# First pair's attention: the high parts of the queries of heads 2 to 7 made by VectorE in place of ScalarE

## The chip, the cores and the metric

One core of a Trainium2 chip runs the whole program. The engines are TensorE (PE in the profile, its weight loads PEld), VectorE (DVE), ScalarE (ACT), GpSimd (POOL) and SyncE (SP), which issues most transfers. The metric is the device time of one execution in microseconds (us), as the median of several.

## The reference

Two blocks follow each other. The first has two layers ("the first pair"), the second two others. Only the attention of the first block is touched. It is a window attention over 512 tokens, in row blocks of 128, with 8 query heads of 64 channels and 2 key heads; each row block sees itself, its neighbours and 256 context rows. In layer 0 the 256 context rows are updated too, so they are two more row blocks of queries.

```python
def window_attention(q, k, v, kc, vc, sink_b):
    ...
        s_loc = jnp.einsum('bqkgd,bnkd->bkgqn', qi, ks).astype(jnp.float32)
        s_loc = jnp.where(valid, s_loc, -jnp.inf)
        s_ctx = jnp.einsum('bqkgd,bnkd->bkgqn', qi, kc).astype(jnp.float32)
        p = sink_softmax(jnp.concatenate([s_ctx, s_loc], axis=-1), sink_b).astype(v.dtype)
        return (jnp.einsum('bkgqn,bnkd->bqkgd', p[..., :nc], vc)
                + jnp.einsum('bkgqn,bnkd->bqkgd', p[..., nc:], vs))
```

Beside the attention each layer has a Fourier mix and a short convolution ("the sides"), which are gated and merged with the attention's output by `w_out`.

## The kernel before

The program is written by hand, one instruction stream for each engine, with semaphores between them. The order of the streams is the order of the code; nothing is scheduled. Matrix products keep nearly fp32 precision: each operand is split into a high part (rounded to the type fp32r) and a low part (the rest), and three products are added. For weights ScalarE makes the high part (`w_hi`, line 874) and GpSimd the low part (`w_lo`, line 800).

In the attention the queries of a head lie on 64 partitions of `q1` (a part of `qk`). For the scores both parts of a head's queries are put in one buffer of 128 partitions, `q_parts[h % 2]`: the high part on its own 64 partitions, the low part on the other 64. There are two such buffers, so head h is written when the scores of head h - 2 are done. A head's queries are 64 x 768 in layer 0 (six row blocks) and 64 x 512 in layer 1 (four).

The attention is a pipeline over steps, one row block of one head (a unit) a step: `n_q` is 6 in layer 0 and 4 in layer 1, so there are 48 and 32 units. At step s TensorE makes the scores of unit s (line 1504), transposes the probabilities of unit s - 3 (line 1523) and multiplies unit s - 4 with the values (line 1539). VectorE at its step st adds mask and takes the minimum for unit st (`scored`, lines 2203 and 2205; TensorE makes the scores of unit s + 2 in the same PSUM region only after it), scales the output of unit st - 5 (line 2224), takes a reciprocal (line 2214), and then does what `side_lo` lists for the step. ScalarE at each step copies the transposed probabilities to `pt` (line 935; TensorE's next transposes use the same PSUM region and wait for it), takes the exponential of a unit (`exp1`, line 922), and then does what `between` lists.

Those two lists are what the change touches. In `between` ScalarE made the high part of head h = step // n_q + 2 at the last step of a head (`q_hi`, line 916), behind a wait for the scores of that step. In `side_lo` VectorE makes the low part of head st // n_q + 1 at the first step of a head (`q_lo`, line 2473), from head 2 on: steps 6, 12, 18, 24, 30, 36 in layer 0, and 4, 8, 12, 16, 20, 24 in layer 1. `SIDE_STEPS` is (10, 14, 18, 22): at these steps ScalarE makes the high part of one side (`h_hi`, line 1163), and two steps later, at 12, 16, 20 and 24, VectorE makes its low part (`h_lo`, line 2191), behind `q_lo` where both fall on a step. At steps 24, 26, 28 and 30 ScalarE also splits weights (`w_hi`), and GpSimd follows with `w_lo`. GpSimd's other work in the attention is the Fourier gate (lines 815 to 822, `fpair` and `gf`), at its start.

Heads 0 and 1 get their parts before the loop, from ScalarE (`q_hi`) and VectorE (`q_lo`), in both kernels.

Of the kernel before, what the change touches and what calls it, by code (L numbers as in the profile page):

```python
# [14 lines left out]
F32 = mybir.dt.float32  # L15
F32R = mybir.dt.float32r
ALU = mybir.AluOpType
# [10 lines left out]
HD = 64  # L28
EPS = 1e-6
HEADS, KVH = 8, 2  # L30
# [104 lines left out]
def _program(nc, I, out, seen):  # L135
    ctx = ExitStack()
    with ctx:
# [216 lines left out]
        s_q0_landed = Signal(nc, ctx, seen, "q0_landed")  # L354
        s_q_hi = Signal(nc, ctx, seen, "q_hi")
        s_q_lo = Signal(nc, ctx, seen, "q_lo")
        s_q_rot = Signal(nc, ctx, seen, "q_rot")
        s_recip = Signal(nc, ctx, seen, "recip")
        s_resid = Signal(nc, ctx, seen, "resid")
# [498 lines left out]
        def _(act):  # L858
# [53 lines left out]
            def q_hi(l, h):  # L912

                b = HD * (h % 2)
                n = TOK if l < DEPTH - 1 else SEQ
                act.activation(q_parts[h % 2][b:b + HD, 0:n], q1[b:b + HD, h // 2, 0:n], ACT.Copy).then_inc(s_q_hi.sem, s_q_hi.nth((l, h)))
# [104 lines left out]
            for l in range(DEPTH):  # L1021
# [125 lines left out]
                exp1(l, units, 3)  # L1147

                def between(step):
                    h = step // n_q + 2  # L1150
                    if step % n_q == n_q - 1 and h < HEADS:
                        act.wait_ge(s_scores.sem, s_scores.at((l, step)))
                        q_hi(l, h)
                    if step == SIDE_STEPS[0]:
                        act.wait_ge(s_fmix.sem, s_fmix.at((l, "ctx") if both else (l, 1)))
                    if step in SIDE_STEPS:
                        c = SIDES[SIDE_STEPS.index(step)]
                        if c < 2:
                            act.wait_ge(s_fgate.sem, s_fgate.at((l, c)))
                        else:  # L1160
                            act.wait_ge(s_side.sem, s_side.at((l, c)))
                        src = gf[:, c, 0:nc_] if c < 2 else cb[:, c - 2, 0:nc_]
                        act.activation(h_hi[:, 4 + c, 0:nc_], src, ACT.Copy).then_inc(s_hi.sem, s_hi.nth((l, "s", c)))
                    if step in (24, 28):
                        split_next((0,))
                    if step in (26, 30):
                        split_next((1,))
# [1008 lines left out]
        def _(dve):  # L2176
            V = nc.vector
# [210 lines left out]
            for l in range(DEPTH):  # L2388
# [80 lines left out]
                def q_lo(h):  # L2469
# [3 lines left out]
                    V.tensor_tensor(q_parts[h % 2][HD - b:2 * HD - b, 0:nc_], q1[b:b + HD, h // 2, 0:nc_],  # L2473
                                    q_parts[h % 2][b:b + HD, 0:nc_].bitcast(F32), ALU.subtract).then_inc(s_q_lo.sem, s_q_lo.nth((l, h)))

                cw, bias = VB[l]["conv_w"], VB[l]["conv_b"]
                for c in range(2):
                    tap = [vec_t[:, cw + 2 * j + c:cw + 2 * j + c + 1] for j in range(3)]
# [42 lines left out]
                def side_lo(st):  # L2521

                    if st == 8:
                        summed_in((5, 7)[l])
                        if l == 1:
                            gate_vector(1)

                    if st > 0 and st % n_q == 0 and st // n_q + 1 < HEADS:
                        q_lo(st // n_q + 1)
                    if st in (2, 3):  # L2530
                        mixed_out(st - 2)
                    if st == 3 and both:
                        dve.wait_ge(s_fmix.sem, s_fmix.at((l, "ctx")))
                        V.tensor_copy(fmix[:, :, SEQ:], ps[:, 2, :].rearrange("p (c n) -> p c n", c=2)).then_inc(s_fm_out.sem, s_fm_out.nth((l, "ctx")))
                    if st - 2 in SIDE_STEPS:
                        c = SIDES[SIDE_STEPS.index(st - 2)]
                        src = gf[:, c, 0:nc_] if c < 2 else cb[:, c - 2, 0:nc_]
                        lo_part(h_lo[:, 4 + c, 0:nc_], src, h_hi[:, 4 + c, 0:nc_], (l, "s", c), (l, "s", c))
# [304 lines left out]
```

## Time and profile before

| | us |
|---|---|
| runs | 1903.93, 1906.1, 1907.13 |
| median | 1906.1 |
| the profiled execution's own time | 1902.68 |
| its span | 1900.4 |
| TensorE busy | 1866.1 |
| ScalarE busy | 820.9 |
| VectorE busy | 794.0 |
| GpSimd busy | 714.5 |

The span goes from the first to the last instruction of the profiled execution; its own time is 2.3 us longer. TensorE's granted clock is 0.998 of full speed over the span. The attention of layer 0 lies between about 242 and 322 us of the span, that of layer 1 between about 540 and 603.

### The profile page before, as it was taken

The page shows a single profiled execution, that of the slowest core. Times are in us where ns is not written, and L with a number is a line of the kernel's source. Part 1 is how long each engine was busy: PE and PEld are TensorE (multiplying, and loading weights), DVE is VectorE, ACT ScalarE, POOL GpSimd, SP SyncE. Part 2 cuts the span into 40 slices and gives each one's busy share as a digit, 9 for nine tenths or more (in the row PEclk, how much of TensorE's full clock was granted, in tenths as well). Part 3 has the DMA queues.
Part 4 walks back from the last instruction along what each step waited for, and adds up shares of the span by engine and source line. Part 5 has one row for each costly group of instructions (what it writes and reads, how often), then busy time and mean ns, then how long its engine had stood idle before and what let it go on. Part 6 is the DMA issues. An engine that isn't in the chain of part 4 may idle for free.

```text
span 1900.4 us, 28008 instructions
## 1 busy us (share of the span) xinstructions
PE 1866.1 (98%) x10996; PEld 1576.8 (83%) x10996; DVE 794.0 (42%) x1801; ACT 820.9 (43%) x1577; POOL 714.5 (38%) x567
## 2 busy tenths in 40 slices
PE   8999999999999999999999999999999999999997
PEld 6888878878878888888988888888888898888886
DVE  4585585276465363775311110056277541111003
ACT  5222386472276474873323222127487342232212
POOL 2433221255512453204544445444420355444452
PEclk9999999999999999999999999999999999999999
DMA  9554412125311233102333333223320232332321
GB/s 328 199 143 147 142 24 68 56 74 175 111 24 54 85 102 119 63 1 90 89 105 95 89 111 111 101 88 97 107 84 1 89 89 89 110 91 90 132 89 44
DMA packets 198321, 185.70 MB, mean 98 GB/s; under 512 B 27246, under 2 KB 165636, under 8 KB 198192
## 3 DMA queue, kind: packets, MB, share of 16 engines
q1 hardware_dynamic: 183640, 172.52, 28.8%
q10 hardware_dynamic: 14552, 11.40, 2.1%
q8 instruction: 89, 1.46, 0.3%
q14 instruction: 40, 0.33, 0.1%
HBM read 179.11 MB, written 5.44 MB: 97 GB/s over the span
## 4 chain that ended last, share of the span: by engine, by line
PE 90%; ACT 3%; DVE 2%; POOL 2%; issue 1%; SPq 1%; DMA 1%; DVEq 0%; ACTq 0%
PE ps L1444 25%; PE ps L1446 24%; PE ps L1445 24%; PE ps L2053 3%; PE ps L1969 3%; PE ps L1504 2%; PE ps L1539 2%; PE ps L1523 2%; PE ps L2071 2%; POOL w_lo L800 2%; PE ps L1465 1%; ACT w_hi L874 1%; DMA raw<-in_w_mod 1%; SPq L768 0%; ACT pt L935 0%
## 5 line engine op out<-in xcount | busy, mean ns | idle before, releaser
L800 POOL TENSOR_TENSOR w_lo<-raw,w_hi 128x512 fp32r<-128x512 f32 (+1 forms) x505 | 667.6, 1353 | 1072.0 <-ACT w_hi L874 1071.9
L874 ACT ACTIVATE w_hi<-raw 128x1024 fp32r<-128x1024 f32 (+3 forms) x255 | 252.1, 1034 | 250.4 <-PE ps L1446 191.0
L1444 PE MATMUL ps<-g_hi,w_lo 128*128 128x512 f32 (+1 forms) x928 | 348.4, 375 | 1.4 <-POOL w_lo L800 1.4
L1445 PE MATMUL ps<-g_lo,w_hi 128*128 128x512 f32 (+1 forms) x928 | 347.5, 374 | 0.0
L1446 PE MATMUL ps<-g_hi,w_hi 128*128 128x512 f32 (+1 forms) x928 | 347.4, 374 | 0.0
L1444 PEld LDWEIGHTS ps<-g_hi,w_lo 128*128 128x128 f32 x928 | 174.7, 188 | 33.7 <-issue 1.7
L1445 PEld LDWEIGHTS ps<-g_lo,w_hi 128*128 128x128 f32 x928 | 174.7, 188 | 31.2
L1446 PEld LDWEIGHTS ps<-g_hi,w_hi 128*128 128x128 f32 x928 | 174.7, 188 | 31.2
L2798 DVE TENSOR_TENSOR tmp_f<-ps,tmp_f 128x512 f32<-128x512 f32 x44 | 30.4, 692 | 370.3 <-PE ps L1446 370.3
L1444 PE MATMUL ps<-h_hi,w_lo 128*128 128x512 f32 (+1 forms) x496 | 177.1, 357 | 2.3 <-DVE h_lo L2191 2.3
L1445 PE MATMUL ps<-h_lo,w_hi 128*128 128x512 f32 (+1 forms) x496 | 174.6, 352 | 0.0
L1446 PE MATMUL ps<-h_hi,w_hi 128*128 128x512 f32 (+1 forms) x496 | 174.5, 352 | 0.0
L1444 PE MATMUL ps<-w_hi,hid_lo 128*128 128x512 f32 x352 | 137.1, 390 | 0.0
L1446 PE MATMUL ps<-w_hi,hid_hi 128*128 128x512 f32 x352 | 136.9, 389 | 0.0
L1445 PE MATMUL ps<-w_lo,hid_hi 128*128 128x512 f32 x352 | 136.9, 389 | 0.0
L1399 ACT ACTIVATE hid_hi<-tmp_f 128x512 fp32r<-128x512 f32 x44 | 27.8, 632 | 237.2 <-DVE tmp_f L2798 237.2
L2756 DVE SCALAR_TENSOR_TENSOR res<-res,ps 128x512 f32<-128x512 f32 x32 | 21.8, 685 | 231.6 <-PE ps L1446 231.4
L1444 PE MATMUL ps<-w_hi,g_lo 128*128 128x512 f32 (+3 forms) x320 | 114.2, 357 | 1.5 <-POOL w_lo L800 1.5
L1446 PE MATMUL ps<-w_hi,g_hi 128*128 128x512 f32 (+3 forms) x320 | 112.0, 350 | 0.0
L1445 PE MATMUL ps<-w_lo,g_hi 128*128 128x512 f32 (+3 forms) x320 | 111.7, 349 | 0.0
L1444 PEld LDWEIGHTS ps<-h_hi,w_lo 128*128 128x128 f32 x496 | 93.8, 189 | 21.0 <-issue 8.8
L1446 PEld LDWEIGHTS ps<-h_hi,w_hi 128*128 128x128 f32 x496 | 93.8, 189 | 12.8
(294 smaller groups left out, 3328.3 us busy)
## 6 DMA issues: line engine op xcount, KB each, us to landing
raw<-in_w_in SPq DMA_DIRECT2D x33, 1024.0 KB, 5.0
raw<-in_w_mod SPq DMA_DIRECT2D x24, 1024.0 KB, 6.5
raw<-in_w_gate SPq DMA_DIRECT2D x44, 512.0 KB, 3.6
raw<-in_w_up SPq DMA_DIRECT2D x44, 512.0 KB, 4.7
raw<-in_w_down SPq DMA_DIRECT2D x22, 1024.0 KB, 4.7
raw<-in_w_out SPq DMA_DIRECT2D x8, 1024.0 KB, 5.3
strips<-bias_rows ACTq DMA_DIRECT2D x18, 256.0 KB, 3.2
raw<-in_w_o SPq DMA_DIRECT2D x4, 1024.0 KB, 4.8
```

Source lines behind the costliest of these rows:

```text
L800: pool.tensor_tensor(w_lo[:, i % SPLIT, a:e], raw_of(what)[:, a:e], w_hi[:, i % SPLIT, a:e].bitcast(F32), ALU.subtract).then_inc(s_tile_lo ...
L874: act.activation(w_hi[:, i % SPLIT, a:b], raw_of(what)[:, a:b], ACT.Copy).then_inc(s_tile_hi.sem, s_tile_hi.nth((what, n)))
L1444: pe.matmul(o, lhs[1], rhs[0], start=first, stop=False)
L1445: pe.matmul(o, lhs[0], rhs[1], start=False, stop=False)
L1446: return pe.matmul(o, lhs[0], rhs[0], start=False, stop=last)
L1504: m = pe.matmul(ps_flat[:, o0 + CTX + col:o0 + CTX + col + k.shape[1]], q, k, start=j == 0, stop=j == len(products) - 1)
L1523: m = pe.transpose(ps_flat[:, o0 + P * j:o0 + P * j + P], s_[:, i % n_b, P * j:P * j + P], ident[:])
L1539: m = pe.matmul(ps_flat[q_, o0:o0 + HD], turned, v, start=j == 0, stop=j == n - 1)
L1969: pe.matmul(ps[:, b, 0:u["n"]], u["q"], u["k"], start=True, stop=True).then_inc(s_scores.sem, s_scores.nth((y, i)))
L2053: m = pe.matmul(ps[:, b, 0:HD], pt2[r % N_P][:, P * j:P * j + P], v, start=j == 0, stop=j == len(u["vs"]) - 1)
L2071: m = pe.transpose(ps[:, b, P * j:P * j + P], probs_of(i)[:, P * j:P * j + P], ident[:])
L2798: V.tensor_tensor(tmp_f[:, 2 + j % 2, :], ps[:, 2 * ((j + 2) % 4) + 1, :], tmp_f[:, j % 2, :], ALU.mult).then_inc(s_glu.sem, s_glu.nth((y, ...
```

## The change

ScalarE no longer makes the high parts of heads 2 to 7, in both layers. VectorE makes them, right ahead of the low part: it waits for the scores of the head before (`s_scores` of unit n_q x (h - 1) - 1), copies the queries to fp32r, waits for its own copy (a new semaphore, `later_q_hi`), and subtracts. The low part was released by ScalarE's semaphore before. The low part's instruction is the same.

```diff
@@ -1147,10 +1148,6 @@
                 def between(step):
-                    h = step // n_q + 2
-                    if step % n_q == n_q - 1 and h < HEADS:
-                        act.wait_ge(s_scores.sem, s_scores.at((l, step)))
-                        q_hi(l, h)
                     if step == SIDE_STEPS[0]:
@@ -2473,6 +2470,16 @@
+                def later_q(h):
+
+                    b = HD * (h % 2)
+                    own, other = slice(b, b + HD), slice(HD - b, 2 * HD - b)
+                    dve.wait_ge(s_scores.sem, s_scores.at((l, n_q * (h - 1) - 1)))
+                    V.tensor_copy(q_parts[h % 2][own, 0:nc_], q1[own, h // 2, 0:nc_]).then_inc(s_later_q_hi.sem, s_later_q_hi.nth((l, h)))
+                    dve.wait_ge(s_later_q_hi.sem, s_later_q_hi.at((l, h)))
+                    V.tensor_tensor(q_parts[h % 2][other, 0:nc_], q1[own, h // 2, 0:nc_],
+                                    q_parts[h % 2][own, 0:nc_].bitcast(F32), ALU.subtract).then_inc(s_q_lo.sem, s_q_lo.nth((l, h)))
@@ -2526,7 +2533,7 @@
                     if st > 0 and st % n_q == 0 and st // n_q + 1 < HEADS:
-                        q_lo(st // n_q + 1)
+                        later_q(st // n_q + 1)
```

VectorE's queue at step 12 of layer 0, where head 3 is prepared; before (`ISA` is the reduction with the mask or the reading of its accumulator; `L2191` is the low part of a side):

```order
L2205 ISA sc,small<-ps,band_first,sinks 128x512
L2205 ISA small 128x1
L2224 TENSOR_SCALAR ao_113<-ps,small 128x64
L2214 RECIPROCAL small<-small 128x1
L2473 TENSOR_TENSOR q_parts_112<-qk,q_parts_112 64x768
L2191 TENSOR_TENSOR h_lo<-cb,h_hi 128x768
L2203 COPY sc<-sinks 128x1
L2205 ISA sc,small<-ps,band_mid,sinks 128x640
```

and of the change (the same lines of code stand 3 lines further up or 7 further down in it):

```order
L2202 ISA sc,small<-ps,band_first,sinks 128x512
L2202 ISA small 128x1
L2221 TENSOR_SCALAR ao_113<-ps,small 128x64
L2211 RECIPROCAL small<-small 128x1
L2478 CAST q_parts_112<-qk 64x768
L2480 TENSOR_TENSOR q_parts_112<-qk,q_parts_112 64x768
L2188 TENSOR_TENSOR h_lo<-cb,h_hi 128x768
L2200 COPY sc<-sinks 128x1
L2202 ISA sc,small<-ps,band_mid,sinks 128x640
```

A CAST of 64x768 stands ahead of the low part; everything behind it, `h_lo` and the reduction of unit 13 first, is one instruction further back.

ScalarE's queue over the steps 10 to 12 of layer 0, before:

```order
L1163 ACTIVATE h_hi<-cb 128x768
L935 ACTIVATE pt<-ps 128x640
L922 ACTIVATE sc,small<-sc,small 128x257
L916 ACTIVATE q_parts_112<-qk 64x768
L935 ACTIVATE pt<-ps 128x512
L922 ACTIVATE sc,small<-sc,small 128x513
```

and of the change:

```order
L1160 ACTIVATE h_hi<-cb 128x768
L936 ACTIVATE pt<-ps 128x640
L923 ACTIVATE sc,small<-sc,small 128x257
L936 ACTIVATE pt<-ps 128x512
L923 ACTIVATE sc,small<-sc,small 128x513
```

The activation that wrote `q_parts` is gone between the exponential of unit 11 and the next `pt`; nothing else moved.

## Rows read from the trace of the kernel before

**Rows 1.** The page's first part: busy us (share of the span) xinstructions of each engine.
```profile
PE 1866.1 (98%) x10996; PEld 1576.8 (83%) x10996; DVE 794.0 (42%) x1801; ACT 820.9 (43%) x1577; POOL 714.5 (38%) x567
```

**Rows 2.** Windows, heads of layer 0: stretch, length, busy of PE, PEld, DVE, ACT, POOL, clock.
```profile
246.71:256.56 9.85, 9.85 (x132) 8.18 (x131) 7.50 (x32) 8.42 (x20) 4.91 (x7) 1.00 0.01 3
256.56:267.66 11.10, 10.04 (x132) 8.23 (x131) 8.81 (x33) 9.07 (x21) 0.00 (x0) 1.00 0.01 2
267.66:277.73 10.07, 10.00 (x132) 8.17 (x131) 7.94 (x33) 9.04 (x21) 0.00 (x0) 1.00 0.01 2
277.73:289.04 11.31, 10.21 (x132) 8.10 (x131) 8.05 (x32) 10.67 (x21) 5.83 (x5) 1.00 0.05 6
289.04:299.14 10.10, 10.10 (x132) 8.24 (x132) 7.64 (x32) 9.20 (x23) 4.24 (x4) 1.00 0.27 102
```

**Rows 3.** Timeline of VectorE, step 12 of layer 0: start us, us, engine, line, operation.
```profile
257.44 0.15 DVE L2214 RECIPROCAL small<-small 128x1 f32<-128x1 f32 x1
257.62 0.95 DVE L2473 TENSOR_TENSOR q_parts<-qk,q_parts 64x768 fp32r<-64x768 f32 x1
258.61 0.96 DVE L2191 TENSOR_TENSOR h_lo<-cb,h_hi 128x768 fp32r<-128x768 f32 x1
...
259.55 0.88 DVE L2205 CUSTOM_DVE_ANT_0 sc<-ps,band_mid,sinks 128x640 f32<-128x640 f32 x1
```

**Rows 4.** Timeline of ScalarE, then TensorE, behind step 12: in brackets idle us and releaser.
```profile
260.46 0.83 ACT L922 ACTIVATE sc<-sc,small 128x641 f32<-128x641 f32 x1 [1.33 <-DVE small L2205]
...
260.77 0.45 PE L1539 MATMUL ps<-v,pt 128*64 128x64 f32 x8 [0.44 <-DVE ao L2224]
...
263.87 0.74 PE L1523 MATMUL ps<-ident,sc 128*128 128x128 f32 x5 [0.62 <-ACT pt L935]
```

**Rows 5.** The tile q_parts: ns least/median/most, first to last start, forms.
```profile
L916 ACT ACTIVATE q_parts<-qk x16: 618/729/842, 220.7 to 583.7; 64x768 fp32r<-64x768 f32 x8, 64x512 fp32r<-64x512 f32 x8
L2473 DVE TENSOR_TENSOR q_parts<-qk,q_parts x16: 685/820/1474, 221.7 to 584.7; 64x768 fp32r<-64x768 f32 x8, 64x512 fp32r<-64x512 f32 x8
```

**Rows 6.** VectorE's operations from SBUF to SBUF: timeline, and a group (busy us, mean ns).
```profile
196.14 1.53 DVE L2482 TENSOR_SCALAR conv_y<-cz,vec_t 128x512 f32<-128x512 f32 x1
...
204.43 0.55 DVE L2482 TENSOR_SCALAR conv_y<-cz,vec_t 128x512 f32<-128x512 f32 x1
205.02 0.75 DVE L2483 SCALAR_TENSOR_TENSOR conv_y<-cz,vec_t,conv_y 128x511 f32<-128x511 f32 x1
...
206.59 0.41 DVE L2482 TENSOR_SCALAR conv_y<-cz,vec_t 128x256 f32<-128x256 f32 x1
...
L2352 DVE TENSOR_SCALAR xn<-res,rstd 128x1024 f32<-128x1024 f32 x3 | 2.1, 750 | 0.0
```

**Rows 7.** Timeline of TensorE behind step 24 of layer 0.
```profile
285.24 0.74 PE L1523 MATMUL ps<-ident,sc 128*128 128x128 f32 x5 [0.83 <-ACT pt L935]
```

**Rows 8.** Timeline of GpSimd and of VectorE at step 30 of layer 0.
```profile
288.23 2.52 POOL L800 TENSOR_TENSOR w_lo<-raw,w_hi 128x512 fp32r<-128x512 f32 x2 [1.04 <-ACT w_hi L874]
...
290.10 1.47 DVE L2473 TENSOR_TENSOR q_parts<-qk,q_parts 64x768 fp32r<-64x768 f32 x1
```

**Rows 9.** Timeline of ScalarE and of TensorE behind step 36 of layer 0.
```profile
303.00 0.36 ACT L935 ACTIVATE pt<-ps 128x256 f32<-128x256 f32 x1
...
303.78 0.60 PE L1523 MATMUL ps<-ident,sc 128*128 128x128 f32 x4
```

**Rows 10.** Timeline of ScalarE, TensorE and GpSimd in layer 1's attention.
```profile
579.42 0.84 ACT L922 ACTIVATE sc<-sc,small 128x641 f32<-128x641 f32 x1 [0.17 <-DVE small L2205]
...
580.50 0.60 ACT L935 ACTIVATE pt<-ps 128x512 f32<-128x512 f32 x1 [0.16 <-PE ps L1523]
...
581.70 0.60 PE L1523 MATMUL ps<-ident,sc 128*128 128x128 f32 x4
...
566.62 0.28 PE L1504 MATMUL ps<-k_lo,q_parts 128*128 128x256 f32 x1 [2.15 <-issue]
...
542.88 1.61 POOL L822 TENSOR_TENSOR gf<-gf,fpair 128x512 f32<-128x512 f32 x1
```

More of the change, by code:

```diff
@@ L356, in _program @@
         s_q_lo = Signal(nc, ctx, seen, "q_lo")
+        s_later_q_hi = Signal(nc, ctx, seen, "later_q_hi")
         s_q_rot = Signal(nc, ctx, seen, "q_rot")
```

## Prediction

> **What bounds the kernel now.** I read the page's first part first. TensorE is busy for 1866.1 us of the 1900.4 us span [rows 1], so an edit on another engine can matter only where TensorE has a gap or can be given one. I then cut the attention of layer 0 at the moments when VectorE starts the first row block of a head and asked for the busy time of each stretch [rows 2]. Every head gives TensorE the same matmuls, and the shortest two of the six heads take 9.85 us: that is TensorE's own time for a head. The others take 11.10, 10.07, 11.31 and 10.10 (the sixth, from step 36, 9.85 as well and not shown again), so the six, 62.28 together, stand 62.28 - 6 x 9.85 = 3.2 us above it. No relief of ScalarE can give back more than that here. VectorE is busy 7.5 to 8.8 us of a head there and ScalarE 8.4 to 10.7: both have room on average, so the question is the order inside a head.
>
> Steps count row blocks: a head has six in layer 0 (heads begin at steps 6, 12, 18, 24, 30 and 36), four in layer 1. The timeline of VectorE at step 12 [rows 3] shows its queue behind the first reduction of the head: a reciprocal, then the low part of the next head's queries (0.95 us from 257.62), the low part of a side input `h_lo` (0.96), and only then the reduction of block 13 at 259.55. Three rows tell what is late next [rows 4]: ScalarE stands idle for 1.33 us for that reduction, TensorE 0.44 us for a scaled output behind it, and 0.62 us for ScalarE's copy `pt`, which stands in ScalarE's queue behind two late exponentials and `h_hi`. This is where head 2's 11.10 us come from (1.25 above 9.85). VectorE's delay is what counts there. ScalarE's 0.84 us for the high part, before 257.40, is followed by idle time.
>
> **The change, part by part.**
> ScalarE loses six instructions of 64x768 and six of 64x512, by the row of `q_parts` up to 0.84 and from 0.62 us [rows 5], about 5.0 and 3.7 us of ScalarE's time. VectorE gets as many casts from SBUF to SBUF, right ahead of the low parts, each with a wait of VectorE for itself between the two. Behind this pair stand the reduction of the next block, and for it ScalarE's exponential and `pt`, and TensorE's transposes. The wait for the scores of the head before costs nothing: VectorE has by then reduced a later block.
>
> No such cast is in the trace. The nearest rows are the one-input operations of VectorE between SBUF and SBUF [rows 6]: 0.55 us for 512 elements and 0.41 for 256, that is 0.14 us for 256 more and 0.69 for 768; another takes 0.75 for 1024, so 0.61 for 768 and 0.48 for 512. From above it is bounded by one element a cycle, as the low parts run: 0.95 [rows 3] for 768 and 0.69 for 512 [rows 5]; from below by the 0.41 of a third of the elements. I take 0.6 and 0.47, since a cast has one input as the rows of 0.55 and 0.75 have. The gap of a dependent pair on VectorE is 0.04 (204.43 + 0.55 to 205.02 in the same rows). So VectorE comes later by about 0.64 less the 0.03 that the low part waited before: 0.6 us in layer 0, 0.5 in layer 1. The Trainium skill (VectorE: DVE Perf Modes, section "The perf-mode tier table") has fp32 copies in SBUF at two elements a cycle and tensor_tensor at one; the rows agree, and an estimate by its figures (some 150 fixed cycles and 384 at 0.96 GHz) gives 0.56 for 768, so the sum would be 0.2 us smaller by it.
>
> What of the 0.6 reaches TensorE, layer 0:
> - Steps 12 and 24: the pair is followed by `h_lo` and everything behind it already is what TensorE waits for (0.62 and 0.83 us for `pt`) [rows 4, 7]. All of it: 2 x 0.6.
> - Step 18: the low part alone follows, but step 20 has another `h_lo`, and the head takes 10.07 already [rows 2]. All of it: 0.6.
> - Step 30: no slack either (10.10). There GpSimd runs `w_lo` from 288.23 to 290.75, and VectorE's low part, issued at 290.10, takes 1.47 in place of 0.95: it stood until about 290.6 [rows 8]. Now the cast stands there instead, and the low part ends at 290.6 + 0.6 + 0.95 = 292.2 in place of 291.57: 0.6.
> - Steps 6 and 36 (9.85, no loss today): at step 36 `pt` ends at 303.36 and the transposes begin at 303.78 [rows 9]; 0.42 of the 0.6 is absorbed, and with a second such gap two blocks on I take 0.25 each.
> Together 1.2 + 0.6 + 0.6 + 0.5 = 2.9 us.
>
> Layer 1: here `pt` of the stage in question began at 580.50 with 0.16 idle before it, behind an exponential begun at 579.42, and ended 0.60 us before the transposes at 581.70 [rows 10]. A delay of 0.5 moves the exponential's end to 580.76, `pt`'s to 581.36: 0.3 left, nothing lost, at step 20 and by the same queue at 8, 12, 16 and 24. At step 4 GpSimd starts the multiplication of `gf` at 542.88 [rows 10], in the stretch where VectorE works on the low part. If GpSimd gets in between cast and low part, VectorE stands for its length, and I put half a chance on 0.4: 0.2. ScalarE's relief gives back a tenth where `pt` waited for the high part's end: -0.1. Sum +3.0 us, against the profiled execution 1902.7 to 1905.7; that execution was 3.4 below the median of the runs, 1906.1, so as a median 1909.1. Nothing later takes it back: TensorE is busy for 98% of the span, and what follows the attention is queued on it.
>
> **A rule that speaks against the change.** The row of 1.53 us for the 512 elements that otherwise take 0.55 [rows 6], and the 1.47, show that VectorE can stand while GpSimd works. The Trainium skill (SBUF — State Buffer, section "Who interferes with whom") says that a copy or cast in the two-port mode and GpSimd exclude each other for a whole instruction. The trace agrees. So the cast is a second chance to stand, at steps 6 and 30 in layer 0 and step 4 in layer 1, where GpSimd works; elsewhere it is idle.
>
> **Rivals.**
> 1. Slower beyond what can be told: the cast runs at one element a cycle, 0.95 + 0.04. Then steps 12, 18, 24 and 30 lose 1.0 each and steps 6 and 36 about 0.65: 5.3, and with step 4 up to 5.9: 1912. It decides from a cast of 0.73 us on, where six steps with 0.13 more each bring the sum to 3.8. For it: the output is another type (fp32r), which no one-input row shows. Against: the input is one. GpSimd can add to it: a stand of 1.0 us (1.53 - 0.55) at each of three steps would give 3.0 + 2 to 3 = 1911 to 1912.
> 2. Absorbed: the slack at steps 18, 6 and 36 is larger than read, and only 12, 24 and 30 lose. With the cast at 0.41 that is 1.3; with ScalarE's relief some 1 us: 1907. Against it stand heads 10.07 and 10.10, which have none.
> 3. Faster: ScalarE is the one that sets the pace (10.67 busy of 11.31 at step 24), and its relief lets `pt` come first. At most 3.2 us, so 1903; beside it TensorE's one gap of 2.15 us in layer 1 (at 566.62, waiting for nothing shown, [rows 10]) may fall away with another timing, 1901 together. Against it: ScalarE idles 1.33 us for VectorE in the same head.
>
> **How the numbers follow.** A change under 0.2% (3.8 us) can't be told from none here: the three runs lie 3.2 apart. Forecast (+1.5 to +4.5): 0.50. Rival 1 (+4.5 to +8): 0.20. Rival 2 (-1 to +1.5): 0.18. Rival 3: 0.12. The time is the forecast's, 1909.1, its own range 1907.6 to 1910.6. Low end 1904.4, between rivals 2 and 3; high end 1913, rival 1 with a little of GpSimd's part. Slower: rival 1 and a third of the forecast, 0.36. Faster: the far half of rival 3 with the spread of the runs, 0.07. The rest, 0.57, is no difference.
>
> **What would show it.** Twelve casts of about 0.6 and 0.47 us on VectorE. Heads of about 10.1 us at steps 6 and 36, 11.7, 10.7, 11.9 and 10.7 between; layer 1's heads unchanged; ScalarE 8.7 us less busy but with longer idle times before the exponential. Casts of 0.95 would bring rival 1. Head 2 at 11.1 or less would make the argument wrong: then VectorE's place in the queue was not what held TensorE.

## The result, and the profile after

The changed kernel takes 1906.42 us in the median of 22 runs (1904.04 to 1911.15), the kernel before 1904.35 us in the median of as many. The ratio is 1.0015, with a 95% interval from 1.0009 to 1.0022: +2.9 us, between 1.7 and 4.2. (The two medians lie only 2.1 us apart. The ratios given here are not quotients of the medians beside them, and a few executions of over 2300 us, one of 3084 us among the 22 of the kernel before and four in runs 2 to 4, are left out of the ratios.) That is under the 0.2% that the forecast called no difference. The profiled execution took 1908.06 us, 1.6 above its kernel's median, that of the kernel before 1902.68, 1.7 below it. Its span is 1905.8 us against 1900.4, so 5.4 us more; where the 2.5 us between the two numbers come from is the second half of this study.

The page's first part, as in [rows 1]:

```profile
PE 1867.8 (98%) x10996; PEld 1578.7 (83%) x10996; DVE 799.4 (42%) x1813; ACT 812.8 (43%) x1565; POOL 715.8 (38%) x567
```

VectorE has 12 instructions and 5.4 us more, ScalarE 12 fewer and 8.1 us less. The group of the cast's line (ns least/median/most, first and last start, forms):

```profile
L2478 DVE CAST q_parts<-qk x12: 398/480/1195, 247.4 to 590.2; 64x768 fp32r<-64x768 f32 x6, 64x512 fp32r<-64x512 f32 x6
```

The undisturbed casts take 0.54 to 0.56 us for 768 elements and 0.40 to 0.42 for 512. The windows of the six heads of layer 0 that the change touches, cut as in [rows 2] (the first is the head at step 6):

```profile
246.45:259.08 12.63, 10.07 (x132) 8.26 (x131) 8.31 (x34) 8.08 (x19) 5.21 (x7) 1.00 0.14 51
259.08:270.77 11.69, 10.03 (x132) 8.23 (x131) 9.36 (x34) 8.03 (x19) 0.00 (x0) 1.00 0.01 2
270.77:280.96 10.19, 10.16 (x132) 8.24 (x131) 8.28 (x34) 8.62 (x20) 0.00 (x0) 1.00 0.01 2
280.96:292.86 11.90, 10.03 (x132) 8.15 (x130) 8.60 (x33) 9.72 (x20) 6.53 (x5) 1.00 0.06 7
292.86:303.56 10.70, 10.08 (x132) 8.32 (x132) 8.22 (x33) 8.42 (x21) 4.39 (x4) 1.00 0.25 95
303.56:313.72 10.16, 9.99 (x132) 8.23 (x131) 7.68 (x32) 7.37 (x18) 0.00 (x0) 1.00 0.01 3
```

Against 9.85, 11.10, 10.07, 11.31, 10.10 and 9.85 before, every head is longer, though TensorE's busy time in a head is within 0.2 us of what it was. The first head is out of line: 2.78 us longer. What happens in the others is seen at step 12. VectorE's timeline, as in [rows 3]:

```profile
260.13 0.56 DVE L2478 CAST q_parts<-qk 64x768 fp32r<-64x768 f32 x1
260.73 0.95 DVE L2480 TENSOR_TENSOR q_parts<-qk,q_parts 64x768 fp32r<-64x768 f32 x1
261.71 0.96 DVE L2188 TENSOR_TENSOR h_lo<-cb,h_hi 128x768 fp32r<-128x768 f32 x1
```

And TensorE's timeline of the changed kernel in layer 0 over the heads at steps 12 to 36; these are all the rows in which it stood idle before a group (idle us and releaser in brackets):

```profile
263.88 0.45 PE L1536 MATMUL ps<-v,pt 128*64 128x64 f32 x8 [1.03 <-DVE ao L2221]
266.97 0.74 PE L1520 MATMUL ps<-ident,sc 128*128 128x128 f32 x5 [0.62 <-ACT pt L936]
285.76 0.45 PE L1536 MATMUL ps<-v,pt 128*64 128x64 f32 x8 [1.03 <-DVE ao L2221]
289.07 0.74 PE L1520 MATMUL ps<-ident,sc 128*128 128x128 f32 x5 [0.84 <-ACT pt L936]
297.31 0.45 PE L1536 MATMUL ps<-v,pt 128*64 128x64 f32 x8 [0.62 <-DVE ao L2221]
307.49 0.45 PE L1536 MATMUL ps<-v,pt 128*64 128x64 f32 x8 [0.17 <-DVE ao L2221]
```

The wait for a scaled output of VectorE was 0.44 us behind step 12 [rows 4] and is 1.03: the cast's 0.59 went to TensorE whole. The wait for ScalarE's `pt` is the same 0.62 as before, and so is that of 0.84 ([rows 7]: 0.83). Behind step 24 the 1.03 us stand in place of two short waits in the kernel before, 0.14 us for `pt` and 0.12 for a scaled output. ScalarE, which the change relieves, stands longer instead, 1.93 us for VectorE's reduction where it stood 1.33 [rows 4]:

```profile
263.57 0.83 ACT L923 ACTIVATE sc<-sc,small 128x641 f32<-128x641 f32 x1 [1.93 <-DVE small L2202]
```

### The profile page after: what moved, and what is told of

Same layout as the page of the kernel before. It is cut to its first block, busy times and chain, and to the rows that moved or that the text cites. A ratio compares the mean times of both kernels' runs of the same rounds, so it can differ in the third digit from the quotient of the medians.

```text
span 1905.8 us, 28008 instructions
## 1 busy us (share of the span) xinstructions
PE 1867.8 (98%) x10996; PEld 1578.7 (83%) x10996; DVE 799.4 (42%) x1813; ACT 812.8 (43%) x1565; POOL 715.8 (38%) x567
## 3 DMA queue, kind: packets, MB, share of 16 engines
q8 instruction: 89, 1.46, 0.3%
## 4 chain that ended last, share of the span: by engine, by line
PE 89%; ACT 3%; DVE 3%; issue 2%; POOL 2%; SPq 1%; DMA 1%; DVEq 0%; ACTq 0%
PE ps L1441 25%; PE ps L1443 24%; PE ps L1442 24%; PE ps L2050 3%; PE ps L1966 3%; PE ps L1501 2%; PE ps L1536 2%; PE ps L1520 2%; PE ps L2068 2%; POOL w_lo L801 2%; PE ps L1462 1%; ACT w_hi L875 1%; DMA raw<-in_w_mod 1%; SPq L769 0%; ACT pt L936 0%
```

## Where the profiled execution's other 2.5 us are

TensorE's timeline in the first head has a stretch in which it waited for nothing that the profile shows, as the one in layer 1 [rows 10], which is in the changed kernel too:

```profile
250.02 0.34 PE L1536 MATMUL ps<-v,pt 128*64 128x64 f32 x5 [2.56 <-issue]
...
572.07 0.28 PE L1501 MATMUL ps<-k_lo,q_parts 128*128 128x256 f32 x1 [2.22 <-issue]
```

Asked for its DMA queues between 247.5 and 248.0 us, the changed kernel shows (queue: packets, MB, share of 16 engines):

```profile
q1 hardware_dynamic: 85, 0.15, 78.9%
q8 instruction: 1, 0.02, 12.0%
```

q1 is here the load of `w_out`, and q8 fetches instructions. It must be TensorE's: the page counts 89 packets and 1.46 MB on it, 16 KB each, and TensorE has 2 x 10,996 instructions, 66 bytes of it for each; no other engine has as many. The Trainium skill (Perfetto Trace Analysis, section "The 4-stage abstract model") says that an instruction is 64 bytes long; that makes 1.41 MB, and the trace agrees to 4%. The packet lies at 247.8 us, and TensorE went on at 250.02, 2.2 us behind it. In the kernel before, the packet of this place came at 236.4, well ahead, and the next at 248.7, when the load had passed; there TensorE has no such stretch. But in layer 1 it came at 564.3 in the kernel before, and TensorE went on at 566.62, 2.3 us later again, and the load of `w_out` was running there too. The experiments below follow this up.

## The experiments

Heads are measured as in the windows above, from VectorE's first row block of a head to the next; "six heads" are those from step 6 to step 42 in layer 0, 62.28 us before and 67.27 in the changed kernel's profile, of which 2.56 are the stretch. The runs of one batch share runs of the kernel before; a time behind "against" is the median of those.

**1. VectorE's casts added, ScalarE's kept.** The kernel before, in which VectorE writes the same high parts once more:

```diff
-                        q_lo(st // n_q + 1)
+                        h = st // n_q + 1
+                        own = slice(HD * (h % 2), HD * (h % 2) + HD)
+                        dve.wait_ge(s_q_hi.sem, s_q_hi.at((l, h)))
+                        V.tensor_copy(q_parts[h % 2][own, 0:nc_], q1[own, h // 2, 0:nc_]).then_inc(s_again.sem, s_again.nth((l, h)))
+                        dve.wait_ge(s_again.sem, s_again.at((l, h)))
+                        q_lo(h)
```

> ScalarE keeps the high parts of heads 2 to 7; VectorE makes them a second time, at the place where the changed kernel makes them. Theory (VectorE's place in its queue is the whole cost): heads of layer 0 as in the changed kernel (about 10.1, 11.7, 10.2, 11.9, 10.7, 10.2 us) or up to 0.2 longer, and 2.4 to 3.0 us above the kernel before. Rival (ScalarE's relief pays for a part of the cast in the changed kernel): heads at steps 24 and 30, where ScalarE splits weights, another 0.5 to 0.8 us longer, and +4 us or more.

Measured: 1905.83 us against 1902.9, ratio 1.0008 (0.9999 to 1.0017). Heads 10.49, 11.69, 10.19, 11.90, 10.69, 10.16, six heads 65.12. From the second head on they are those of the changed kernel within 0.01, so all of its loss is there with ScalarE still doing its part. (It is the heads that show it; the interval of the ratio just reaches 1.) The first head shows what the stretch had hidden in the changed kernel: +0.64, not +0.22.

**2. The other half alone: neither engine makes the high parts.**

```diff
                     dve.wait_ge(s_scores.sem, s_scores.at((l, n_q * (h - 1) - 1)))
-                    V.tensor_copy(q_parts[h % 2][own, 0:nc_], q1[own, h // 2, 0:nc_]).then_inc(s_later_q_hi.sem, s_later_q_hi.nth((l, h)))
-                    dve.wait_ge(s_later_q_hi.sem, s_later_q_hi.at((l, h)))
```

> The high parts of heads 2 to 7 are left out altogether; VectorE makes low parts from what stands in the buffers. ScalarE has its relief, VectorE its old load. Theory: heads of layer 0 stay at 9.85, 11.1, 10.0, 11.2, 10.0, 9.85, at most 0.5 us in all below the kernel before. Rival (ScalarE sets the pace): heads at steps 24 and 30 fall to about 9.9, and the kernel is 1.5 to 3 us faster than before.

Measured: 1904.3 us, ratio 1.0002 (0.9993 to 1.0012). The windows of the heads at steps 12 and 24:

```profile
257.38:268.48 11.10, 10.02 (x132) 8.23 (x131) 8.80 (x34) 8.03 (x19) 0.00 (x0) 1.00 0.01 2
...
278.54:289.86 11.32, 10.03 (x132) 8.16 (x131) 8.04 (x33) 9.72 (x20) 5.95 (x5) 1.00 0.05 7
```

ScalarE is busy for 1.04 and 0.95 us less than in the same heads of [rows 2], and they last the same 11.10 and 11.32. Six heads: 62.26. The relief of ScalarE is worth nothing in layer 0, and the third rival falls.

**3. The pair four steps later.** The changed kernel, in layer 0 with cast and low part at st % 6 == 4, where no other low part stands except at step 16's side:

```diff
-                    if st > 0 and st % n_q == 0 and st // n_q + 1 < HEADS:
+                    if st >= n_q and st % n_q == (4 if both else 0) and st // n_q + 1 < HEADS:
```

> The changed kernel, but in layer 0 cast and low part stand four steps later in VectorE's queue (steps 10, 16, ... 40), where VectorE waited 0.9 us for scores. The same instructions. Theory (place, not work): heads of 9.85 to 10.1 us, but about 10.6 for the one at step 12, whose step 16 has a side's low part too; 1.5 to 2.5 us faster than the kernel before, 4 to 5 faster than the changed one. Rival (VectorE's and ScalarE's load itself, wherever it stands): heads as long as in the changed kernel, +2 to +3 against before.

Measured: 1902.8 us, ratio 0.9993 (0.9983 to 1.0003). Heads 10.99, 10.60, 10.09, 11.00, 9.85, 9.86, six heads 62.39; the first holds a stretch of 0.93 without a releaser, so 61.46 without it, 3.6 under the changed kernel's 65.1. So place matters and not work. The gain over the kernel before was put too high: 0.8 us in the heads in place of 1.5 to 2.5, with 11.00 us at step 24, where TensorE waits 0.94 us for `pt`. And since the low parts moved together with the casts, this run alone doesn't give the price of the casts in the new place; run 7 beside run 4 does.

**4. The low parts spread, ScalarE keeps the casts.** The kernel before with the line of run 3, and the sides' low parts at 12, 18, 24 and 30:

```diff
-                    if st - 2 in SIDE_STEPS:
-                        c = SIDES[SIDE_STEPS.index(st - 2)]
+                    low_steps = (12, 18, 24, 30) if both else (12, 16, 20, 24)
+                    if st in low_steps:
+                        c = SIDES[low_steps.index(st)]
```

> The kernel before (ScalarE makes the high parts), in layer 0 with the queries' low parts four steps later and the sides' low parts at steps 12, 18, 24 and 30, so that no step has two long operations of VectorE. Theory: all heads 9.85 to 10.0 but the one at step 24, in which ScalarE has 10.67 us of work and which can't go under about 10.4; 2 to 3 us faster than the kernel before. Rival: the heads at steps 12 and 24 keep their 11.1 and 11.3, because ScalarE's queue and not VectorE's held TensorE, and the time is that of before within 0.5 us.

Measured: 1901.69 us, ratio 0.9992 (0.9981 to 1.0002). Heads 9.84, 10.60, 9.84, 10.81, 9.98, 9.87, six heads 60.94, 1.3 under before and not the 2 to 3 that I had expected. Of what steps 12 and 24 take above 9.85, 1.25 and 1.46 us before, 0.75 and 0.96 stay: TensorE still waits 0.72 and 0.63 us for `pt`, which stands in ScalarE's queue behind `h_hi` and `w_hi`. That part is set by ScalarE's queue, so the rival was in part right.

**5. The change in layer 1 alone.**

```diff
+                    h = step // n_q + 2
+                    if both and step % n_q == n_q - 1 and h < HEADS:
+                        act.wait_ge(s_scores.sem, s_scores.at((l, step)))
+                        q_hi(l, h)
...
-                        later_q(st // n_q + 1)
+                        (q_lo if both else later_q)(st // n_q + 1)
```

> The change in layer 1 alone: in layer 0 ScalarE makes the high parts as before. Theory (all of the loss is made in layer 0, one for one where VectorE had no idle time): layer 0's heads as before, 9.85, 11.10, 10.07, 11.31, 10.10, 9.85 within 0.1; layer 1's heads 7.3 to 7.7 as before, apart from the stretches of one to three microseconds in which TensorE waits for nothing that the profile shows, and the time within 2 us of the kernel before. Rival (ScalarE's relief in layer 1 is worth 0.1 to 0.4 a head): a head or two of layer 1 under 7.25.

A single execution: 1904.48 us, beside 1903.72. Six heads of layer 0: 62.28, exactly as before. In layer 1 7.27, 7.57, (10.86 and 10.18 with a stretch of 3.04 in them), 7.57, 7.56. Nothing is lost at layer 1's steps; the last head is 0.15 shorter than the 7.71 before.

**6. Every cast twice.**

```diff
                     V.tensor_copy(q_parts[h % 2][own, 0:nc_], q1[own, h // 2, 0:nc_]).then_inc(s_later_q_hi.sem, s_later_q_hi.nth((l, h)))
                     dve.wait_ge(s_later_q_hi.sem, s_later_q_hi.at((l, h)))
+                    V.tensor_copy(q_parts[h % 2][own, 0:nc_], q1[own, h // 2, 0:nc_]).then_inc(s_later_q_hi.sem, s_later_q_hi.nth((l, h, 1)))
+                    dve.wait_ge(s_later_q_hi.sem, s_later_q_hi.at((l, h, 1)))
```

> The changed kernel with every cast of VectorE made twice, so that each head's start has one more of 0.40 to 0.56 us. Theory (once the slack is used up, every further microsecond of VectorE goes to TensorE one for one): the heads at steps 12, 24 and 30 another 0.5 to 0.6 longer, 12.3, 12.5 and 11.3; that at step 18, which had hidden 0.5 of the first cast, now loses nearly all of the second, 10.7; those at steps 6 and 36 0.5 to 0.6, 10.6 and 10.7; layer 1 loses little (under 0.5 a head). In all 3 us over the changed kernel, 5 to 6 over the one before, ratio 1.003. Rival (slack or the wait of TensorE is something else that does not scale): heads as in the changed kernel, and the ratio stays at 1.0015.

Measured: 1913.24 us, ratio 1.0042 (1.0027 to 1.0057), more than expected. Heads 11.24, 12.28, 10.77, 14.88, 10.92, 10.76. Steps 12, 18 and 36 came as expected (+0.59, +0.58, +0.60). Step 6 gave a little more (+0.75 on 10.49), step 30 less, +0.22 in place of some 0.6: the casts there take 0.84 and 0.55 us ahead of GpSimd's `w_lo`, in place of one of 1.20 behind it. Step 24 was missed by 2.4 us. Its timeline and windows (us, busy of PE, PEld, DVE, ACT, POOL, granted clock):

```profile
285.46 3.51 POOL L801 TENSOR_TENSOR w_lo<-raw,w_hi 128x512 fp32r<-128x512 f32 x2 [31.44 <-ACT w_hi L875]
285.93 1.92 DVE L2188 TENSOR_TENSOR h_lo<-gf,h_hi 128x768 fp32r<-128x768 f32 x1
...
289.06 0.69 PE L1536 MATMUL ps<-v,pt 128*64 128x64 f32 x8 [2.58 <-DVE ao L2221]
...
289.06:294.06 5.00, 5.00 (x31) 4.15 (x31) 2.93 (x14) 3.98 (x9) 2.25 (x2) 0.50 0.00 0
```

Pushed back by 0.6 us, VectorE's side part ran into GpSimd's `w_lo` and took 1.92 us in place of 0.94; TensorE stood for 2.58 us, and the clock granted in the 5 us behind it was 0.50, the lower of its two levels (1.2 GHz). The prediction had GpSimd idle at step 24, though [rows 2] has it busy for 5.83 us of that head; in the changed kernel `w_lo` starts 2.76 us into the head (283.72) and `h_lo` just ahead of it (283.60), so that it still took 0.96. In layer 1 the same came at step 4: the low part took 1.65 us beside GpSimd's `gf` in place of 0.69, and the head 7.85 in place of 7.28. So a second cast is not a second 0.6 us everywhere: it can move a neighbour into GpSimd's way, and what TensorE then loses is more than the wait.

**7. Both orders spread, VectorE makes the high parts.** The changed kernel with the edits of runs 3 and 4.

> The changed kernel with both orders of layer 0 spread: a head's high and low part on VectorE four steps later, and the sides' low parts at steps 12, 18, 24 and 30. Theory (what costs is that several pieces of VectorE stand in one step, not their sum): heads between 9.85 and 10.7, in all 60.5 to 61.5 for steps 6 to 42 against 62.3 before and 64.7 in the changed kernel, the time 1 to 3 us under the changed kernel and 1 us or so under the one before, ratio 0.999. Rival (VectorE's cast costs its 0.5 us wherever it stands): heads 0.5 longer each than with ScalarE's cast in the same places, 64 in all.

Measured: 1902.71 us, ratio 0.9991 (0.9982 to 1.0000). Heads 9.85, 10.60, 9.85, 10.99, 9.85, 9.85, six heads 60.99, with ScalarE's casts in the same places (run 4) 60.94. Who makes the high part is worth 0.05 us then. The head at step 24, 10.99, is above the 10.7 that I had allowed. What was left at step 12 is the same wait for `pt`:

```profile
263.13 0.74 PE L1520 MATMUL ps<-ident,sc 128*128 128x128 f32 x5 [0.72 <-ACT pt L936]
```

**8. The changed kernel once more**, unaltered.

> The changed kernel once more, unaltered, for a second profile of it. Theory (the stretch of 2.56 us at 250.02 in which TensorE waits for nothing that the profile shows belongs to that execution, not to the change): the head at step 6 is 10.1 without it, 10.1 to 12.6 with one of another length, and the other heads repeat within 0.05: 11.69, 10.19, 11.90, 10.70, 10.16. Rival (the change itself makes that stretch): again 2.5 us at the same place.

A single execution: 1909.16 us. Five heads repeat within 0.02 (11.69, 10.17, 11.91, 10.69, 10.18). But the stretch is there again, in the same place of the program, so the theory as I had put it ("belongs to that execution") fell:

```profile
251.06 0.34 PE L1536 MATMUL ps<-v,pt 128*64 128x64 f32 x5 [2.03 <-issue]
```

The instruction packet can be followed through all traces. There are 13 such stretches over 0.5 us in the ten traces with the old order of SyncE's queue (before, changed, runs 1 to 8): one in layer 1 in each, and in layer 0 those of the changed kernel, of run 8 and of run 3. Ahead of each stands a packet of q8, 0.5 to 1.3 us before the `w_out` load has landed, and TensorE goes on 2.2 to 2.5 us after it: 247.8 and 250.02; 248.7 and 251.06; 246.2 and 248.52; in layer 1 564.3 and 566.62, 569.7 and 572.07, 570.7 and 573.24, and so on. The seven traces without a stretch in layer 0 have a packet between 235.9 and 239.7; the three with one have none from 225 us to the late one. Counted in matmuls and weight loads, TensorE stops at the same place of its program each time, behind the 3,203rd in layer 0 and the 7,863rd in layer 1, and the packet is the same one, the 12th and the 31st on q8. So the packet is late, and the candidate was what stands on SyncE's queue there: the gate rows, 2048 packets of 4 bytes in layer 0 and 1024 in layer 1, and 1024 KB of `w_out` behind them, landing 13 to 16 us after its issue.

**9. The load ahead of the gate rows.** The changed kernel, with one block of SyncE moved:

```diff
-                if what[1:] == ("out", 1, 0):
-                    l = what[0]
-                    sp.wait_ge(s_gate_vec.sem, s_gate_vec.at(l))
-                    for s in range(2 - l):
-                        sp.dma_start(gate_rows[l, s].rearrange("(c p) -> p c", p=P), mod_g[:, s, :], allow_slow_non_contiguous=True).then_inc(s_gate_row.sem, s_gate_row.nth(l, 16))
...
                 for into, src in loads:
                     sp.dma_start(into(raw[:, n % RAW, :]), src).then_inc(landed_sems[n % RAW], 16)
+                if what[1:] == ("out", 1, 0):
+                    l = what[0]
+                    sp.wait_ge(s_gate_vec.sem, s_gate_vec.at(l))
+                    for s in range(2 - l):
+                        sp.dma_start(gate_rows[l, s].rearrange("(c p) -> p c", p=P), mod_g[:, s, :], allow_slow_non_contiguous=True).then_inc(s_gate_row.sem, s_gate_row.nth(l, 16))
```

> The changed kernel with one more edit: on SyncE's queue the second 1024 KB of w_out is asked for ahead of the gate rows (packets of 4 bytes, 1024 a row) in place of behind them. In the changed kernel's two profiles TensorE's stretch without a releaser at step 7 (2.56 and 2.03 us) ends 2.3 us after a packet of TensorE's instruction queue, and that packet stands in the last microsecond of this load; in the kernels without the stretch the packet came earlier or after the load. Theory (the load behind the small packets keeps back TensorE's next instructions): the load lands some 5 us after its issue, and no such stretch over 0.5 us stands in layer 0; that of layer 1 (1.9 to 3.0 in all profiles) goes too or gets shorter; time 0 to 3 us under the changed kernel, ratio 0.9995 to 1.0015. Rival (the small packets alone keep it back, or the load does wherever it stands): stretches as before, in another place, ratio 1.0015.

Measured: 1901.97 us against 1903.06, ratio 0.9990 (0.9981 to 0.9999), under the range that I had expected: the order of the queue is worth more than the change costs. No stretch is left in either layer. In layer 1, 10 us windows around the place, of the changed kernel and then of this run:

```profile
570.00:580.00 10.00, 7.93 (x87) 6.80 (x86) 5.41 (x19) 4.53 (x11) 0.00 (x0) 0.83 0.01 3
```

```profile
565.00:575.00 10.00, 10.00 (x137) 8.75 (x138) 7.37 (x30) 8.32 (x19) 0.00 (x0) 1.00 0.01 2
```

One thing beside the order changed: in layer 1 SyncE now asks for the load before it waits for the gates, at 527.2 us in place of 556.3, so it has long landed when the small packets go out at 553.6. In layer 0 the load is asked for at 231.4 in place of 234.3 and takes 11.5 us, not the 5 that I had expected. The small packets alone still slow TensorE's packet in layer 1, which took 3.4 us in place of 0.9, but it came at 560.6 and in time. SyncE's timeline, of the changed kernel and then of this run:

```profile
556.25 0.58 SPq L769 DMA_DIRECT2D raw<-in_w_out  x1
```

```profile
527.22 0.37 SPq L764 DMA_DIRECT2D raw<-in_w_out  x1
```

The stretch costs more than its 2.2 us: behind it the granted clock falls (0.83 in the mean of the window), and two heads take 10.42 and 9.15 us; here they take 7.58 and 7.56, 4.4 us less. Layer 0's heads, 10.48, 11.69, 10.17, 11.91, 10.67 and 10.16, are now free of the stretch and give the change's own price. VectorE's two instructions at step 6 are disturbed by GpSimd in this run as in the changed kernel:

```profile
247.44 0.71 DVE L2478 CAST q_parts<-qk 64x768 fp32r<-64x768 f32 x1
248.18 1.23 DVE L2480 TENSOR_TENSOR q_parts<-qk,q_parts 64x768 fp32r<-64x768 f32 x1
```

**10. The gate rows in long runs.** The changed kernel with the old order of the queue:

```diff
-                        sp.dma_start(gate_rows[l, s].rearrange("(c p) -> p c", p=P), mod_g[:, s, :], allow_slow_non_contiguous=True).then_inc(s_gate_row.sem, s_gate_row.nth(l, 16))
+                        sp.dma_start(gate_rows[l, s].rearrange("(p c) -> p c", p=P), mod_g[:, s, :], allow_slow_non_contiguous=True).then_inc(s_gate_row.sem, s_gate_row.nth(l, 16))
```

> The changed kernel, with the gate rows stored in runs of 32 bytes (128 packets a row in place of 1024), which leaves out the transposition of the gates: their values stand in another order. Theory (the 2048 small packets of layer 0 and 1024 of layer 1 are what makes the w_out load take 15 us and keeps back TensorE's instructions): the load lands in some 5 us; no stretch of TensorE over 0.5 us without a releaser in either layer, heads of layer 0 as in the changed kernel otherwise, 10.1, 11.7, 10.2, 11.9, 10.7, 10.2; the profiled span 4 to 5 us under the changed kernel's 1905.8; ratio 0.9990 to 1.0005. Rival (the stretches are something else): they stand as before, 2 to 3 us each, ratio 1.0015.

Measured: 1901.85 us, ratio 0.9993 (0.9984 to 1.0002), span 1899.1 against 1905.8; no stretch, heads 10.47, 11.69, 10.17, 11.90, 10.69, 10.17. The landing of layer 1's `w_out` load, in the changed kernel and then here:

```profile
DMA to landing us min/median/max: 14.5/14.5/14.5
```

```profile
DMA to landing us min/median/max: 4.9/4.9/4.9
```

In layer 1 the load still stands right behind the gate rows (issued at 554.0), but these are an eighth of the packets; the load is three times as fast, and TensorE's packet is in time. In layer 0 that load took 8.1 us in place of 14.8. That separates the small packets from the load's place: it is they that hold the queue up. Whether by their number or by their size is not separated, since a row has the same 4 KB in both.

**11. The spread order and the load ahead.** The kernel before with the edits of runs 4 and 9.

> The kernel before with VectorE's low parts spread in layer 0 as in the run of that name (pairs four steps later, sides at steps 12, 18, 24 and 30), and the w_out load ahead of the gate rows. Theory (both gains add): heads of layer 0 60.9 in all for steps 6 to 42, no stretch of TensorE without a releaser in layer 1, so 1.3 and up to 2.2 us under the kernel before: ratio 0.9982 to 0.9993. Rival (the order of the load is worth nothing): ratio 0.9992 as with the spread alone, a stretch of 1.3 to 3 us in layer 1.

Measured: 1897.51 us (1897.0 to 1898.65) against 1903.06, ratio 0.9965 (0.9952 to 0.9977), better than expected and the fastest here. Its ratio is that of run 12, though, so what the spread order adds is seen in the spans alone, 1895.3 us against 1896.3. Six heads 60.91, layer 1's heads 7.28, 7.57, 7.56, 7.57, 7.57, 7.69. It beats both kernels.

**12. The kernel before with the load ahead alone.**

> The kernel before, with the w_out load ahead of the gate rows and nothing else. Both sides of the change then stand without TensorE's stretches: this kernel and the changed one with the same order of the load. Theory (the change costs VectorE's casts where they stand, 2.8 us over the six heads, and what else the profiled executions showed between the kernels was the late packet): heads of layer 0 62.3 for steps 6 to 42 against 65.1 with the change, layer 1 45.2 in both, no stretch over 0.5 us; the time 1899.0 to 1899.8, ratio 0.9976 to 0.9986, that is 2.4 to 3 us under the changed kernel with the same load order. Rival (the change's cost was partly the late packet, so that less is left without it): the two within 1.5 us of each other, this one over 1900.5.

Measured: 1898.67 us (1898.56 to 1899.83) against 1905.8, ratio 0.9965 (0.9952 to 0.9979); six heads 62.30, layer 1's 45.3 as expected, the time a little under the expected range. Against run 9 the profiled spans are 1896.3 and 1899.2, 2.9 us apart, the medians 1898.67 and 1901.97, 3.3 apart (on two chips). Taken against the kernel before of their own batches, 0.9990 and 0.9965, they are nearly 5 us apart, each with an interval of some 2 us to either side; the profiles are the firmer measure. With the late packet out of the way on both sides, their 2.9 us are what the change costs.

## Why the prediction was right

The forecast was +3.0 us and measured was +2.9 (1.7 to 4.2); without the late packets 2.9 in the profiles. The time itself, 1906.42 us, lies inside the full range of 1904.4 to 1913 but under the forecast's own 1907.6 to 1910.6: the 3.0 had been added to 1906.1, the median of three executions, and with 22 that kernel's median is 1904.35. Point by point:

- **The cast's price.** Taken as 0.6 and 0.47 us, measured 0.54 to 0.56 and 0.40 to 0.42 undisturbed. The first rival's one element a cycle (0.95) did not come. By the Trainium skill (VectorE: DVE Perf Modes, section "The perf-mode tier table") the estimate was 0.56; the trace agrees, for an output in fp32r too.
- **Steps 12 and 24**: 0.6 each forecast, +0.59 and +0.59 measured, by the mechanism named; but the wait that grew is TensorE's for VectorE's scaled output (to 1.03, from 0.44 at step 12 and 0.12 at step 24), not the one for `pt` that the prediction rested on, which stayed at 0.62 and 0.84.
- **Step 30**: 0.6 forecast, +0.60 measured, by the working given: the cast stands behind GpSimd's `w_lo`, the low part behind it runs free.

```profile
293.80 1.20 DVE L2478 CAST q_parts<-qk 64x768 fp32r<-64x768 f32 x1
295.03 0.95 DVE L2480 TENSOR_TENSOR q_parts<-qk,q_parts 64x768 fp32r<-64x768 f32 x1
```

- **Step 18**: 0.6 forecast, +0.12 measured. The step "the head takes 10.07 already, all of it" was mis-sized: a head that is 0.2 us above the shortest can still have slack at its start. In the kernel before VectorE's reduction of block 20 waited 0.25 us for the scores, by a row that the prediction did not read:

```profile
271.23 0.88 DVE L2205 CUSTOM_DVE_ANT_0 sc<-ps,band_mid,sinks 128x640 f32<-128x640 f32 x1 [0.25 <-PE ps L1504]
```

In the changed kernel the same reduction, at 274.45, follows its predecessor without idle time. Counted from the start of the head, the cast begins 0.12 us earlier than the low part did, so the reduction of block 19 is 0.46 us later (2.57 in place of 2.11) and that of block 20 only 0.11 (3.68 in place of 3.57); that much the head lost. The second cast of run 6, when the slack was used up, cost 0.58 in this head.
- **Steps 6 and 36**: 0.25 each forecast. Step 36 gave +0.31, by the same slack as at step 18 (the reduction of block 38 had waited 0.26 us for scores) and a wait of 0.17 for a scaled output, not by the slack before the transposes behind `pt`, from which the 0.25 was taken. Step 6 gave +0.63 (10.49, 10.48 and 10.47 in runs 1, 9 and 10), because beside GpSimd's `fpair` the cast took 0.71 and the low part 1.23. Rival 1's addition "GpSimd can add to it" came there, in a small measure. In the changed kernel's own profile this head shows +0.22 besides the stretch, since some of VectorE's delay lies inside the stretch.
- Together: 0.63 + 0.59 + 0.12 + 0.59 + 0.60 + 0.31 = 2.84, forecast 2.9. With the two effects in layer 1 below it is 3.0. Step 18 was set 0.5 too high and step 6 0.4 too low; that the sum fits so well is in part luck. So is the 3.0 for the whole kernel, in which 0.35 us in layer 1 stand that nobody forecast.
- **Layer 1**: -0.1 forecast for ScalarE's relief and +0.2 for GpSimd at step 4. The last head went from 7.71 to 7.56 (-0.15), step 4's stayed at 7.27: no stand there with one cast, though there was one with two (run 6). One thing was not foreseen: at the start of layer 1 VectorE's `k_lo` begins 0.45 us after its releaser ended in place of 0.10, and TensorE waits 1.08 us in place of 0.72. After, then before:

```profile
539.58 0.55 DVE L2505 TENSOR_TENSOR k_lo<-qk,k_twice 64x384 fp32r<-64x384 f32 x1 [4.72 <-ACT k_twice L1109]
```

```profile
534.26 0.55 DVE L2498 TENSOR_TENSOR k_lo<-qk,k_twice 64x384 fp32r<-64x384 f32 x1 [4.36 <-ACT k_twice L1108]
```

It is in the changed kernel and in runs 3, 7, 8, 9 and 10 and in no other. Nothing in the trace names it, and it stays open.
- **Rival 2** (absorbed) held at one step of six. **Rival 3** (faster) fell by runs 1 and 2. Its second half, that the 2.15-us gap of layer 1 may go with another timing, had the right object and the wrong cause: no timing of the twelve casts removed it, the order on SyncE's queue did.
- **The size of the profiled difference** (5.4) would have looked like rival 1. It is 2.4 in the six heads, 2.56 of the stretch and 0.35 of the `k_lo`, less 0.15 in layer 1's last head; with the start 0.3 us earlier, 0.24 us more between the layers and 0.17 in layer 1's two heads behind the stretch this leaves the 5.3 us by which layer 1's last head ends later. Whether the unprofiled runs had the stretch in layer 0 can't be seen. Their +2.9 says that most had not, or that the kernel before paid as often elsewhere.

## What to carry to other kernels

A light instruction moved to a less busy engine cost its full length here where that engine's queue is what the bottleneck waits for, a part of it where there is some idle time behind it, and nothing where there is enough; the same six casts cost 2.8 us at a head's start and 0.05 us four steps later with the sides moved too. Read the slack of each place from the idle time before the next instruction of that engine, not from the length of the stage. And where the bottleneck has a gap that no engine explains, look for its instruction packets on the DMA queues and at what was queued ahead of them: moving five lines on SyncE's queue gave 4 to 7 us here (spans 1900.4 to 1896.3 and 1905.8 to 1899.2), the spread order of VectorE 1.3.

## What the hardware showed unexpectedly

- TensorE's instructions come in packets of 16 KB over the DMA engines that also move data. In 13 of 13 stretches it went on 2.2 to 2.5 us after a packet that was late. Late it was only with 1024 or 2048 packets of 4 bytes ahead of a 1024 KB load; in none of the four traces with another order or with longer runs. Why the packet passed in time in layer 0 in seven of the ten others was not found.
- The spread of the runs went with it: 1.3 to 1.8 us in each of runs 9 to 12 (5 to 11 executions), against 6 to 7 us in 22 each of the kernel before (without one of 3084 us) and the changed one, and 6.4 in the 11 of run 7.
- A stand of TensorE of 2.6 us (run 6) was followed by 5 us at half the granted clock; one of 2.2 us in layer 1 by a window at 0.83, while that of 2.56 us in layer 0 was followed by none (1.00), and so was another of 2.22 us in layer 1, that of run 7. The length of the stand alone doesn't decide it; what does is not shown here.
